# Raw tokens for sixteen units of the Hgrn projection, the norm's factor on their banks, and a new order in the fox stage

## The reference

```python
h = rms_norm_2(x, norm_g[l]) * (1.0 + scale[:, None, :]) + shift[:, None, :]
# even mixer
proj = (h @ w_in).astype(jnp.float32)          # 3072 columns: q, f, i, g_a, u, g_b
forget = lb + (1.0 - lb) * jax.nn.sigmoid(f)
logf, key = jnp.log(forget), 1.0 - forget
o_a = hgrn2_chunked(q, key, i, logf)           # chunks of 64 in the reference
# odd mixer: proj = h @ w_in, and logf = log_sigmoid(fl + b_f), cumulated over the tokens
```

## Time and profile before

| | us |
|---|---|
| median of 3 runs | 1333.59 |
| the profiled execution | 1333.02 |
| its span, first to last instruction | 1331.2 |
| PE busy, share of the span | 98% |
| DVE, ACT, POOL busy | 70%, 61%, 8% |
| mean granted TensorE clock | 1.00 |

### The profile page before, as it was taken

One profiled execution on the slowest core, in us unless ns is written; L12 is line 12 of the kernel. 1 busy time (PEld: TensorE's weight loads), 2 busy tenths in 40 slices (PEclk: granted clock), 3 DMA queues, 4 the chain that ended last, 5 costly groups with the idle time before them and its releaser, 6 DMA issues.

```text
span 1331.2 us, 28040 instructions
## 1 busy us (share of the span) xinstructions
PE 1309.0 (98%) x10496; PEld 1279.5 (96%) x10496; DVE 927.4 (70%) x1526; ACT 810.9 (61%) x1582; POOL 109.6 (8%) x120
## 2 busy tenths in 40 slices
...
DMA packets 64580, 240.54 MB, mean 181 GB/s; under 512 B 7840, under 2 KB 9360, under 8 KB 64496
## 3 DMA queue, kind: packets, MB, share of 16 engines
...
...
HBM read 237.70 MB, written 1.05 MB: 179 GB/s over the span
## 4 chain that ended last, share of the span: by engine, by line
PE 88%; DVE 6%; ACT 4%; issue 1%; DMA 1%; SPq 0%; POOL 0%; ACTq 0%; POOLq 0%; DVEq 0%
PE bank L2042 26%; PE bank L2044 25%; PE bank L2043 25%; DVE w_lo L1244 2%; PE bank L2086 1%; PE bank L2093 1%; PE bank L2094 1%; ACT w_hi L665 1%; PE bank L2425 1%; DVE h L1314 1%; DVE arena L1308 1%; PE bank L2409 1%; PE bank L2408 1%; PE bank L2410 1%; ACT x_hl L706 0%
## 5 line engine op out<-in xcount | busy, mean ns | idle before, releaser
L1244 DVE TENSOR_TENSOR w_lo<-raw,w_hi 128x1024 fp32r<-128x1024 f32 (+2 forms) x376 | 490.3, 1309 | 217.6 <-ACT w_hi L665 217.4
L2042 PE MATMUL bank<-x_hl,w_hi 128*128 128x272 f32 (+1 forms) x2000 | 577.1, 289 | 3.6 <-ACT arena L1148 2.3
L2044 PE MATMUL bank<-x_hl,w_lo 128*128 128x272 f32 (+1 forms) x2000 | 572.4, 286 | 0.0
L2043 PE MATMUL bank<-x_hl,w_hi 128*128 128x272 f32 (+1 forms) x2000 | 570.0, 285 | 0.0
L665 ACT ACTIVATE w_hi<-raw 128x1024 fp32r<-128x1024 f32 (+2 forms) x376 | 409.6, 1096 | 132.4 <-PE bank L2044 117.3
L2042 PEld LDWEIGHTS bank<-x_hl,w_hi 128*128 128x128 f32 x2000 | 376.5, 188 | 4.9 <-issue 2.9
L2043 PEld LDWEIGHTS bank<-x_hl,w_hi 128*128 128x128 f32 x2000 | 379.1, 190 | 0.4
L2044 PEld LDWEIGHTS bank<-x_hl,w_lo 128*128 128x128 f32 x2000 | 375.9, 188 | 0.0
L2042 PE MATMUL bank<-a_hi,w_hi 128*128 128x272 f32 (+2 forms) x968 | 277.6, 287 | 0.3 <-ACT vn L925 0.2
L2044 PE MATMUL bank<-a_hi,w_lo 128*128 128x272 f32 (+2 forms) x968 | 275.8, 285 | 0.0
L2043 PE MATMUL bank<-a_lo,w_hi 128*128 128x272 f32 (+2 forms) x968 | 275.3, 284 | 0.0
...
## 6 DMA issues: line engine op xcount, KB each, us to landing
...
```

Source lines behind the costliest of these rows:

```text
L1244: ve.tensor_tensor(w_lo[:, s, cols], raw[:, s, cols], w_hi[:, s, cols].bitcast(F32), ALU.subtract).then_inc(w_lo_ready, 1)
L2042: te.matmul(dst, w_hi[:, s, a:a + P], rhs_hi, start=first, stop=False)
L2043: te.matmul(dst, w_hi[:, s, a:a + P], rhs_lo, start=False, stop=False)
L2044: return te.matmul(dst, w_lo[:, s, a:a + P], rhs_hi, start=False, stop=last)
```

## The change

Units 0 to 15 of ein take raw tokens, as the first four of oin did. ein_quad replaces first_quad: it starts when the first pair of h is updated; VectorE updates all chunks in pairs (ein_update); POOL adds four of the squares together (add0, add1) and four ones-matmuls stand in ein_quad before the last lower part. VectorE applies r_t to each bank and copies the bias column (hg_factor), ScalarE works from there with the bias (hg_biased). The normalised tokens that the token units need are made later, chunk by chunk: hg_normed, hg_normed_upper (at the units of NORM_AT = {6: 0, 7: 1, 9: 2, 10: 3, 11: 4, 12: 5, 13: 6, 14: 7}), hg_normed_lower. hg_tokens waits for the last of them (xl7). In the fox stage: the shift's lower part (sl) two steps earlier; behind_quad asks for the third unit's weights after eight matmuls; its ones-matmuls at k == 3; the logit matmuls wait chunk by chunk; exp and ln at u == 4, the cumulation at u == 5; four casts behind the loop. At the program's start the squares stand one split later. The declared orders of the steps (vec.phase, act.phase and so on) follow; those hunks are left out, and all lines are moved 12 columns to the left.

```diff
@@ -865,11 +872,12 @@
-for s in range(SLOTS):
-    if s:
-        split_hi("gu0", 0, s)
-    square("pre0", 2 * s)
-    square("pre0", 2 * s + 1)
+for s in range(1, SLOTS):
+    split_hi("gu0", 0, s)
+    square("pre0", 2 * s - 2)
+    square("pre0", 2 * s - 1)
+square("pre0", 6)
+square("pre0", 7)
@@ -1005,16 +1013,28 @@
+sc.wait_ge(vec.sem, vec.at("pree", "gs"))
+sc.activation(raw_shift[0], mod[:, 0, 0, :].unsqueeze(2).broadcast_to([P, DC, COL]), ACT.Copy
+              ).then_inc(act.step("pree", "sh"), 1)
...
-for c in SQ_ORDER["pree"]:
-    if c >= 5:
-        pre_square("pree", c, (pool.sem, pool.at("res3", f"h{c}")))
-    else:
-        pre_square("pree", c, (vec.sem, vec.at("res3", h_step(c))))
-pre_rms("pree")
-for c in range(DC):
-    pre_upper("pree", c)
-sc.preload_act_table(ACT.Sigmoid)
...
+def ein_upper(c):
+    sc.wait_ge(vec.sem, vec.at("pree", f"h{c - c % 2}"))
+    sc.activation(raw_x[c][0][:, 0:SEQ], h[:, c, META:T], ACT.Copy, scale=gs[:, 0, c:c + 1]).then_inc(act.step("pree", f"b{c}"), 1)
...
+def ein_square(c):
+    pre_square("pree", c, (vec.sem, vec.at("pree", f"h{c - c % 2}")))
...
+for c in (0, 2, 4):
+    ein_upper(c)
+    ein_upper(c + 1)
+    ein_square(c)
+    ein_square(c + 1)
+ein_square(6)
+ein_square(7)
+ein_upper(6)
+ein_upper(7)
+rsqrt("pree", STAT[:, 0:SEQ], r_t[:, 0:SEQ], 1.0 / D, eps6, (pe.sem, pe.at("pree", "ss")))
@@ -1022,21 +1042,32 @@
 def hg_split(v):
     split_next("ein", v // SLOTS - 1, v % SLOTS)
-def hg_evict(v):
-    hg_done(v)
-    func = ACT.Sigmoid if v < 4 else ACT.Copy if v < 8 else ACT.Silu
-    sc.activation(hg[HG_PLACE[v]], bank[HG_BANK[v]][:, 0:SEQ], func).then_inc(act.step("hg", f"e{v}"), 1)
-
-for v in range(3):
-    hg_split(v + 4)
-    hg_evict(v)
-hg_evict(3)
+def hg_biased(v):
+    sc.wait_ge(vec.sem, vec.at("hg", f"w{v}"))
+    func = ACT.Sigmoid if v < 4 else ACT.Identity if v < 8 else ACT.Silu
+    sc.activation(hg[HG_PLACE[v]], hg[HG_PLACE[v]], func, bias=hg_bias[:, v:v + 1]).then_inc(act.step("hg", f"e{v}"), 1)
+
+def hg_normed_upper(c):
+    sc.wait_ge(vec.sem, vec.at("hg", f"xt{c}"))
+    sc.activation(x_hi[:, c, 0:SEQ], xt[:, c % 2, 0:SEQ], ACT.Identity, bias=mod[:, 0, 0, c:c + 1]
+                  ).then_inc(act.step("hg", f"xh{c}"), 1)
+
+hg_split(4)
+hg_split(5)
+sc.preload_act_table(ACT.Sigmoid)
+hg_biased(0)
+hg_biased(1)
+hg_split(6)
+hg_biased(2)
 hg_split(7)
-for v in range(4, 16):
+hg_biased(3)
+for v in range(4, HG_RAW):
     if v == 8:
         sc.preload_act_table(ACT.Silu)
-    hg_evict(v)
     hg_split(v + 4)
+    hg_biased(v)
+    if v in NORM_AT:
+        hg_normed_upper(NORM_AT[v])
 sc.preload_act_table_set("natural_log_exp_and_others")
 sc.wait_ge(pe.sem, pe.at("hg", f"lv{LEVELS}"))
 sc.activation(xt[:, :, 0:256], bank[5][:, :].rearrange("p (a b) -> p a b", a=2), ACT.Copy
@@ -1190,7 +1221,7 @@
-    if u == 3:
+    if u == 4:
@@ -1645,16 +1676,35 @@
+ve.scalar_tensor_tensor(gs[:, 0, :], mod[:, 0, 1, :], 1.0, par("norm_g", 0, 8), ALU.add, ALU.mult
+                        ).then_inc(vec.step("pree", "gs"), 1)
...
+def ein_update(c):
+    cs = slice(c, c + 2)
+    ve.tensor_tensor(f[:, cs, 0:SEQ], f[:, cs, 0:SEQ], r_t[:, 0:SEQ].unsqueeze(1).broadcast_to([P, 2, SEQ]), ALU.mult
+                     ).then_inc(vec.step("pree", f"t{c}"), 1)
+    own("pree", f"t{c}")
+    ve.tensor_tensor(h[:, cs, META:T], f[:, cs, 0:SEQ], h[:, cs, META:T], ALU.add).then_inc(vec.step("pree", f"h{c}"), 1)
...
+def ein_lower(c):
+    ve.wait_ge(act.sem, act.at("pree", f"b{c}"))
+    hi, lo = raw_x[c]
+    ve.scalar_tensor_tensor(lo[:, 0:SEQ], h[:, c, META:T], gs[:, 0, c:c + 1], hi[:, 0:SEQ].bitcast(F32),
+                            ALU.mult, ALU.subtract).then_inc(vec.step("pree", f"bl{c}"), 1)
...
-for c in (0, 1, 2):
-    normed("res3", c, SEQ)
-    added("res3", c, slice(META, T), SEQ)
-ve.tensor_tensor(f[:, 4, 0:SEQ], f[:, 4, 0:SEQ], r_t[:, 0:SEQ], ALU.mult).then_inc(vec.step("res3", "t4"), 1)
-own("res3", "t4")
-ve.tensor_tensor(h[:, 4, META:T], f[:, 4, 0:SEQ], h[:, 4, META:T], ALU.add).then_inc(vec.step("res3", "h4"), 1)
+ein_update(0)
+ve.wait_ge(act.sem, act.at("pree", "sh"))
+ve.tensor_tensor(raw_shift[1], mod[:, 0, 0, :].unsqueeze(2).broadcast_to([P, DC, COL]),
+                 raw_shift[0].bitcast(F32), ALU.subtract).then_inc(vec.step("pree", "sl"), 1)
+for c in (2, 4, 6):
+    ein_update(c)
+    ein_lower(c - 2)
+    ein_lower(c - 1)
+ein_lower(6)
+ein_lower(7)
...
-pre("pree")
@@ -1662,6 +1712,27 @@
+def hg_factor(v):
...
+    if v == 0:
+        ve.wait_ge(act.sem, act.at("pree", "r"))
+    ve.wait_ge(unit_done, SLOTS * FIRST_QUAD["ein"] + v + 1)
+    ve.tensor_tensor(hg[HG_PLACE[v]], bank[HG_BANK[v]][:, 0:SEQ], r_t[:, 0:SEQ], ALU.mult).then_inc(vec.step("hg", f"m{v}"), 1)
+    ve.tensor_copy(hg_bias[:, v:v + 1], bank[HG_BANK[v]][:, SEQ:SEQ + 1]).then_inc(vec.step("hg", f"w{v}"), 1)
...
+def hg_normed(c):
...
+    if c >= 2:
+        own("hg", f"xl{c - 2}")
+    ve.scalar_tensor_tensor(xt[:, c % 2, 0:SEQ], h[:, c, META:T], gs[:, 0, c:c + 1], r_t[:, 0:SEQ], ALU.mult, ALU.mult
+                            ).then_inc(vec.step("hg", f"xt{c}"), 1)
...
+def hg_normed_lower(c):
...
+    ve.wait_ge(act.sem, act.at("hg", f"xh{c}"))
+    ve.scalar_tensor_tensor(x_lo[:, c, 0:SEQ], xt[:, c % 2, 0:SEQ], mod[:, 0, 0, c:c + 1], x_hi[:, c, 0:SEQ].bitcast(F32),
+                            ALU.add, ALU.subtract).then_inc(vec.step("hg", f"xl{c}"), 1)
@@ -1679,17 +1750,34 @@
     own("hg", f"fm{h_}")
     ve.tensor_tensor(hg[28 + h_], hg[h_], hg[4 + h_], ALU.mult).then_inc(vec.step("hg", f"q{h_}"), 1)
+hg_factor(0)
+hg_factor(1)
 hg_split(4)
+hg_factor(2)
 hg_split(5)
 hg_forget(0)
+hg_forget(1)
+hg_factor(3)
 hg_split(6)
-hg_forget(1)
 hg_forget(2)
+hg_forget(3)
+hg_factor(4)
 hg_split(7)
-hg_forget(3)
-for v in range(4, 8):
-    hg_split(v + 4)
-    hg_query(v - 4)
+hg_query(0)
+hg_factor(5)
+hg_split(8)
+hg_query(1)
+hg_factor(6)
+hg_normed(0)
+hg_split(9)
+hg_query(2)
+hg_factor(7)
+hg_normed_lower(0)
+hg_normed(1)
+hg_split(10)
+hg_query(3)
+hg_split(11)
+hg_factor(8)
 hg_split(12)
 ve.wait_ge(pe.sem, pe.at("hg", "dg"))
 own("hg", "q3")
@@ -1736,6 +1824,10 @@
         hg_scores(i - 1)
     hg_split(13 + i)
     tot = hg_level(i, tot)
+    hg_factor(9 + i)
+    hg_normed_lower(1 + i)
+    if 2 + i < DC:
+        hg_normed(2 + i)
 hg_scores(LEVELS - 1)
 def hg_gated(c):
@@ -1813,14 +1905,14 @@
+ve.wait_ge(act.sem, act.at("preo", "sh"))
+ve.tensor_tensor(raw_shift[1], mod[:, 1, 0, :].unsqueeze(2).broadcast_to([P, DC, COL]),
+                 raw_shift[0].bitcast(F32), ALU.subtract).then_inc(vec.step("eout2", "sl"), 1)
...
-ve.wait_ge(act.sem, act.at("preo", "sh"))
-ve.tensor_tensor(raw_shift[1], mod[:, 1, 0, :].unsqueeze(2).broadcast_to([P, DC, COL]),
-                 raw_shift[0].bitcast(F32), ALU.subtract).then_inc(vec.step("eout2", "sl"), 1)
@@ -1831,11 +1923,6 @@
-ve.tensor_copy(ident_c, ident).then_inc(vec.step("fl0", "ib"), 1)
...
@@ -1855,7 +1942,7 @@
-    if u == 4:
+    if u == 5:
@@ -1875,6 +1962,11 @@
...
+ve.tensor_copy(ident_c, ident).then_inc(vec.step("fl0", "ib"), 1)
...
@@ -2018,11 +2110,13 @@
-gp.wait_ge(act.sem, act.at("res3", "r"))
-for c in (5, 6, 7):
-    gp.tensor_tensor(f[:, c, 0:SEQ], f[:, c, 0:SEQ], r_t[:, 0:SEQ], ALU.mult).then_inc(pool.step("res3", f"t{c}"), 1)
-    gp.wait_ge(pool.sem, pool.at("res3", f"t{c}"))
-    gp.tensor_tensor(h[:, c, META:T], f[:, c, 0:SEQ], h[:, c, META:T], ALU.add).then_inc(pool.step("res3", f"h{c}"), 1)
+for i in range(2):
+    gp.wait_ge(vec.sem, vec.at("pree", "h6"))
+    gp.wait_ge(act.sem, act.at("pree", "sq5"))
+    if i:
+        gp.wait_ge(pool.sem, pool.at("pree", "add0"))
+    gp.tensor_tensor(sq8[:, 0:2, 0:SEQ], sq8[:, 0:2, 0:SEQ], sq8[:, 2 + 2 * i:4 + 2 * i, 0:SEQ], ALU.add
+                     ).then_inc(pool.step("pree", f"add{i}"), 1)
@@ -2386,16 +2480,45 @@
-pre("pree", SQ_ORDER["pree"])
-keep_clock(8, bank[3])
-first_quad("pree", "ein", SEQ, (bank[0], bank[1], bank[2]))
...
-        te.wait_ge(act.sem, act.at("hg", f"e{v - 6 if v < 12 else v - 4}"))
-    unit("ein", bank[HG_BANK[v]], v % SLOTS, SEQ)
+        te.wait_ge(vec.sem, vec.at("hg", f"w{v - 6 if v < 12 else v - 4}"))
+    for k in range(DC):
+        last = product(bank[HG_BANK[v]][:, 0:SEQ + COL], v % SLOTS, k, *raw_x[k], k == 0, k == DC - 1)
+    last.then_inc(unit_done, 1)
...
+def ein_quad():
...
+    n, q = SEQ + COL, FIRST_QUAD["ein"]
+    te.wait_ge(w_lo_ready, SLOTS * q + 3)
+    te.wait_ge(vec.sem, vec.at("pree", "sl"))
...
+    def lower(k):
+        te.wait_ge(vec.sem, vec.at("pree", f"bl{k}"))
+        for u in range(3):
+            last = te.matmul(bank[u][:, 0:n], w_hi[:, u, k * P:(k + 1) * P], raw_x[k][1], start=False, stop=k == DC - 1)
+            if k == DC - 1:
+                last.then_inc(unit_done, 1)
...
+    for k in range(DC):
+        te.wait_ge(act.sem, act.at("pree", f"b{k}"))
+        for u in range(3):
```

(52 more changed lines are left out.)

20 lines of the change are left out of this document (13 added, 7 removed).

## The result

The changed kernel takes 1336.98 us in the median of 14 runs (1335.75 to 1337.84), the kernel before 1333.63 beside it (14 runs): ratio 1.0022, interval 1.0015 to 1.0029, so 3.35 us slower (2 to 4 by the interval). 1333.6 was forecast, with a range from 1329.5 to 1337.0. The profiled execution took 1337.12 us.

A forecast was written before the change was run, and what follows sets the result against it. TensorE, busy for 98% of the span, was taken as the bound. The terms -0.6 - 6.4 + 0.5 + 1.1 + 0.3 + 3.0 + 4.5 - 2.4 gave 0.0 us, so 1333.6 us, range 1329.5 to 1337.0.

The forecast's parts named there:

- the entry that does not move: Rival at ein's entry: something else holds the first matmul, the 6.4 us gain shrinks to about 3, 1337 us; chance 0.04.
- the fox order: Fox stage: the reordered steps remove most of TensorE's two stops of 1.9 and 1.7 us, -2.4 us in sum.
- Entry with POOL's additions: Entry of ein: product matmuls start earlier, -6.4 us; POOL's two additions of squares make the norm late, +0.5 us.
- Levels: Level steps: VectorE and ScalarE wait on each other, 5.48 us a step against TensorE's 4.71, +3.0 us.
- Stop: Behind the last level: TensorE waits for unit 15's activation and the last lower half before the token units, +4.5 us.
- Theory A: Experiments' theory: VectorE's and ScalarE's mutual waits in the level steps and the late token block are on the path.
- The clock falls: Rival behind the last level: TensorE's idle stop halves its clock, costing 2.2 us once, 1335.8 us; chance 0.20.
- The second stop: Fox stage: TensorE's stop for a ScalarE operation standing behind exp and ln goes when these move after it, -1.7 us.
- 0.7 stay: Fox stage, before behind_quad: of 1.8 us gained, 1.1 turn into a wait before unit 4 and 0.7 remain.
- The start: Program's start: two squares no longer stand before the split of slot 1, -0.6 us.
- VectorE as the bound from unit 4: Rival in ein's units from 4 on: VectorE's small reserve is used up and it bounds the kernel, 1335.7 us; chance 0.08.
- The ring that doesn't bind: Rival in the level steps: VectorE's and ScalarE's mutual waits don't hold TensorE, 1328.3 us; chance 0.14.

The follow-up runs named there:

- the run with the ring opened: Changed kernel with ScalarE's next weight split ahead of the normalised token's upper part in the level steps: 1332.77 us, ratio 0.9992.
- the two edits: On the changed kernel, separately: ScalarE's next split ahead of the normalised token's upper part, 1332.77 us; factor 15 and last lower part ahead of VectorE's last level step, 1333.12 us.
- the fillers: Changed kernel with 19 ones-matmuls into a free bank in TensorE's stop behind the last level matmul: 1334.14 us, ratio 1.0002.
- both edits and fillers: Changed kernel with ScalarE's next split ahead of the upper part, factor 15 ahead of the last level step, four ones-matmuls behind the last level: 1327.87 us, ratio 0.9959.

## Why the prediction was right or wrong

**The total.** The forecast was 1333.6 us and the measured median is 1336.98, 0.02 us inside the upper end of the range. Of the rivals only the entry that does not move reached 1337, and the entry moved as forecast; so it is luck that the range held. In the profile two terms make most of the miss, and they are nearly of one size: the clock (+1.84, put at nothing in the sum) and the fox order (-0.75 for -2.4, +1.65).

**The even part was worked out right, to 0.3 us a step, but for the clock.** Entry with POOL's additions: -5.9 forecast, -6.13 measured. The additions took 1.42 and 1.28 us, not 1.9, and neither the 0.5 us nor the upper end of 1.1 came; VectorE paid for them instead (four lower halves 3.76 us beside POOL, two of them 0.88 without), where TensorE hardly waited:

```profile
1057.42 3.76 DVE L1692 SCALAR_TENSOR_TENSOR a_lo<-h,gs,a_hi 128x256 fp32r<-128x256 f32 x4
```
```profile
1057.63 1.42 POOL L2118 TENSOR_TENSOR arena<-arena 128x512 f32<-128x512 f32 x1 [15.96 <-DVE h L1687]
1059.22 1.28 POOL L2118 TENSOR_TENSOR arena<-arena 128x512 f32<-128x512 f32 x1 [0.17 <-ACT a_hi L1023]
```

Units 3 to level 0: +0.9 forecast with their share of the columns, +1.1 measured. Levels: +3.0 and 0.5 of columns forecast, +3.50 measured, and the run with the ring opened gave 2.95 of it back. Stop: +4.5 forecast, +4.59 measured. Theory A is shown by the two edits.

**The step that failed: the rival "The clock falls", at "Clock 0.20", with nothing for it in the sum.** I set the chance low, with the argument that stops up to 1.9 us did nothing. It happened on top of the forecast's stop in every profile that had 1.29 us or more there and no fillers (1.4, 1.5, 1.8 and 2.7 us), and the fillers took it away: 1.8 us of the block; the median fell by 2.8, with the fox stage's scatter in it. My price of 2.2 us lies among these; the rival gave 1335.8. The forecast itself had a stop of 4.5 us, so this rival belonged beside it with more than half of the chance. The forecast's own last sentences asked for a granted clock of 1.00 behind the stop, and it was 0.50. The Trainium skill (TensorE: Matmul & The Clock Gate, "Part 1: The HAM clock gate") says that an idle array falls back to half its clock. The trace agrees, 0.50 for 6.8 us. I had weighed it below one row of another place.

**The fox order was over-sized: -2.4 forecast, -1.8 alone.** The second stop went whole (-1.7, as forecast). Of the first, "0.7 stay" failed: in the profile of the fox order alone 0.3 stay, in the changed kernel unit 4 comes 0.9 later than before, counted from the even mixer's last sums. I wrote that the time of the split before unit 4 "hangs on r_t and VectorE and hardly moves". The change itself moves it: its ones-matmuls stand at k == 3, 4.1 us behind the quad's start in the profile of the fox order alone (1.9 before, 5.2 in the changed kernel, where the third unit waits) and 1.1 us after the last square in the profile with both edits and fillers, and the norm loop, split and first factor hang on that. And the third unit's weights were assumed there in time. In six of ten profiles with the new order the transfer that its split waits behind came 0.6 to 1.05 us late, in none of three without it; it is issued before anything that the order moves, so I take that for chance, but no run tested it.

**The start**, -0.6 forecast, gave 0.4 in the medians, and that is not told from nothing.

**Rivals that fell.** VectorE as the bound from unit 4: TensorE has no stop there before the diagonal. The ring that doesn't bind: it did. The entry that doesn't move: it did by 6.1 us.
